# Outer buffers for three expert pairs, two single-use buffers, router rows in two blocks, and the pool scale spread by GpSimd

## What is computed

```python
def pool_mixer(x, pool_w, pool_scale):     # layer 0
    ...
    y = jnp.einsum("bsgc,gcd->bsgd", pooled, pool_w).reshape(B, S, D)
    return y * pool_scale                  # one factor for each of 2048 features

def hier_moe(...):                         # in both layers, 16 experts
    # router: top-1 group of 4, then top-2 of its 4 experts
    h = silu(einsum("td,edf->tef", xt, w_gate)) * einsum("td,edf->tef", xt, w_up)
    y = einsum("tef,efd->td", h * gate[:, :, None], w_down)
```

## Time and profile before

| | |
|---|---|
| median of 3 runs | 1384.12 us (1383.57 to 1386.93) |
| profiled execution, span | 1384.6 us |
| TensorE (PE) busy | 1344.2 us, 97% |
| VectorE (DVE) busy | 556.2 us, 40% |
| ScalarE (ACT) busy | 412.7 us, 30% |
| GpSimd (POOL) busy | 42.2 us, 3% |
| DMA | 481.80 MB, mean 348 GB/s |
| mean granted TensorE clock | 0.990 |

### The profile page before, as it was taken

How to read it: one execution, slowest core, us unless ns; L and a number is a source line. 1 busy time by engine, 2 the same in 40 slices (tenths; PEclk the granted TensorE clock), 3 DMA queues, 4 the chain that set the end, 5 groups by cost and what they waited for, 6 DMA issues and landing times.

```text
span 1384.6 us, 21994 instructions
## 1 busy us (share of the span) xinstructions
PE 1344.2 (97%) x9081; PEld 763.4 (55%) x9081; DVE 556.2 (40%) x906; ACT 412.7 (30%) x636; POOL 42.2 (3%) x35
## 2 busy tenths in 40 slices
PE   9899999999999999999999999999999999999997
PEld 8644444443334458888888877764444444334443
DVE  5813222232222246566665665552322323222223
ACT  5611111111101136665656565531111111111112
POOL 1200000000000000000000000110000000000000
PEclk9999999999999999999999999999999999999999
DMA  9999999999999999644545444579999999999997
GB/s 361 406 421 421 419 421 421 426 427 428 428 428 423 421 394 384 209 157 156 179 141 193 152 152 152 183 263 421 420 421 421 421 426 428 427 428 428 424 420 269
DMA packets 86657, 481.80 MB, mean 348 GB/s; under 512 B 6462, under 2 KB 6672, under 8 KB 47412
## 3 DMA queue, kind: packets, MB, share of 16 engines
q1 hardware_dynamic: 85988, 477.50, 85.7%
q10 hardware_dynamic: 432, 2.65, 0.5%
q0 software_dynamic: 160, 0.52, 0.1%
HBM read 478.56 MB, written 2.10 MB: 347 GB/s over the span
## 4 chain that ended last, share of the span: by engine, by line
issue 53%; PE 34%; DMA 7%; DVE 3%; POOL 1%; ACT 1%; SPq 1%; POOLq 0%; ACTq 0%; DVEq 0%
PE ps L1789 13%; PE ps L1597 7%; DMA ring<-in_moe_w_up 6%; PE ps L1827 5%; PE ps L1678 2%; PE ps L1843 2%; PE ps L1754 1%; PE ps L1755 1%; POOL head_rs L625 1%; DMA bias_row<-in_moe_b_rt 1%; DVE ws L1024 1%; PE ps L1882 1%; PE ps L1816 0%; DVE ps L1354 0%; DVE resid L1357 0%
## 5 line engine op out<-in xcount | busy, mean ns | idle before, releaser
L1789 PE MATMUL ps<-ring,xg 128*64 128x512 f32 x1664 | 388.2, 608 | 19.8 <-DMA ring<-in_moe_w_up 15.4
L1597 PE MATMUL ps<-ws,xs 128*128 128x512 f32 x1632 | 383.8, 393 | 2.6 <-DVE ws L1027 1.1
L1597 PEld LDWEIGHTS ps<-ws,xs 128*128 128x128 f32 x1632 | 304.0, 189 | 70.9 <-DVE ws L1027 3.6
L1789 PEld LDWEIGHTS ps<-ring,xg 128*64 128x64 f32 x1664 | 123.0, 139 | 255.0 <-issue 254.7
L1827 PE MATMUL ps<-ring,hidT 128*64 128x512 f32 x832 | 184.6, 595 | 0.0
L1027 DVE SCALAR_TENSOR_TENSOR ws<-ring,vecs,ws 128x512 fp32r<-128x512 f32 x192 | 134.3, 747 | 87.5 <-ACT ws L646 87.5
L1221 DVE TENSOR_TENSOR y_lo<-ps,y_hi 64x512 fp32r<-64x512 f32 x112 | 77.1, 688 | 191.6 <-ACT y_hi L710 188.9
L646 ACT ACTIVATE ws<-ring,vecs 128x512 fp32r<-128x512 f32 x192 | 127.3, 715 | 83.1 <-PE ps L1597 83.0
L1201 DVE TENSOR_TENSOR resid<-resid,ps 128x512 f32<-128x512 f32 x112 | 72.0, 684 | 170.8 <-PE ps L1755 170.8
L701 ACT ACTIVATE silu_g<-ps,slot_scale 64x512 f32<-64x512 f32 x28 | 19.1, 684 | 402.3 <-PE ps L1789 402.3
L710 ACT ACTIVATE y_hi<-ps 64x512 fp32r<-64x512 f32 x112 | 66.3, 592 | 209.2 <-PE ps L1827 207.2
(11 more groups left out here) (199 smaller groups left out, 825.0 us busy)
## 6 DMA issues: line engine op xcount, KB each, us to landing
ring<-in_moe_w_gate SPq DMA_DIRECT2D x72, 1024.0 KB, 13.9
ring<-in_moe_w_up SPq DMA_DIRECT2D x72, 1024.0 KB, 14.7
ring<-in_moe_w_down SPq DMA_DIRECT2D x72, 1024.0 KB, 15.0
ring<-in_moe_w_gate SPq DMA_DIRECT2D x24, 2048.0 KB, 15.7
ring<-in_moe_w_up SPq DMA_DIRECT2D x24, 2048.0 KB, 20.1
ring<-in_moe_w_down SPq DMA_DIRECT2D x24, 2048.0 KB, 18.5
ring<-in_w_kv SPq DMA_DIRECT2D x32, 1024.0 KB, 5.7
ring<-in_w_q SPq DMA_DIRECT2D x16, 1024.0 KB, 5.4
```

Of the source, the lines that this page charges most:

```text
L1597: last = mm(ps[:, bank + t, :], xs[:, px, k, cols], ws[:, b, pw, j, :], start=(first and j == 0 and n == 0), stop=(last_unit and j == 1 an ...
L1789: last = mm(ps[CAP * h:CAP * h + CAP, b, :], xg[:, b, k, :], both[h][:, j, :], start=(k == 0), stop=(k == KD - 1))
```

## The change

The outer buffers are used for three pairs (`PEELED` = 3, 72 loads). Two further buffers, `early`, take loads 6 and 7 of the layer, once; they lie at 0 to 8 KB and 16 to 24 KB, where `xs` holds the high and low half of the first eight tiles, and wait until these have been read (layer 0: four units used; layer 1: 28 of the O product's 32). The first round is thus 19 loads; loads 19 to 24 take the buffers of 0 to 5, load 25 that of load 8, and so on 17 back. The three outer buffers in `ws` wait each for its own last use. The fifth outer buffer (load 18) waits for the residual in layer 0 and is issued last of the first round; in layer 1 it is issued first, as soon as the third chunk of `oT` has been split. `xr` shrinks to 8 tiles, used alternately by blocks 0, 2 and 1, 3. `xg` and `y_hi` change places, `pick` moves. The pool scale comes by one DMA of 8 KB to one partition (`scale_src`), and GpSimd spreads each group over the partitions with `partition_broadcast`, at the places where it issued DMAs; the spreads of groups 0 and 1 stand behind the first norm's power.

```diff
-PEELED = 2
+PEELED = 3
...
+FIRST = WIDE + EARLY
+EARLY_LOADS = (6, 7)
+ROUND = [m for m in range(FIRST) if m not in EARLY_LOADS]
+BEFORE = {m: m - WIDE if m - FIRST >= WIDE else ROUND[m - FIRST] for m in range(FIRST, AHEAD)}
...
+OLD_XR = 18
+ISSUE_ORDER = [[0, 1, 2, 3, 4, 5, 8, 9, 10, 11, 12, *EARLY_LOADS, 13, 14, 15, 16, 17, OLD_XR],
+               [OLD_XR, 0, 1, 2, 3, 4, 5, 8, 9, 10, 11, 12, *EARLY_LOADS, 13, 14, 15, 16, 17]]
...
-        xr = at(56 * KB, "xr", [P, KD, SEQ])
+        xr = at(56 * KB, "xr", [P, 8, SEQ])
+        xr_all = at(56 * KB, "xr_all", [P, KD, SEQ])
...
-        xg = at(0, "xg", [P, 2, KD, CAP])
-        y_hi = at(8 * KB, "y_hi", [P, NBLK, BLK], F32R)
+        y_hi = at(0, "y_hi", [P, NBLK, BLK], F32R)
+        xg = at(8 * KB, "xg", [P, 2, KD, CAP])
...
+        early = [at(16 * KB * j, f"early{j}", [P, 2048]) for j in range(EARLY)]
...
+        EXTRA_BUFS = [extra[:, j, :] for j in (1, 2, 0, 3, 4)] + [early[j][:, :] for j in range(EARLY)]
+        LAST_UNITS = (UNIT_ATT, UNIT_O + 8 * NBLK)
+        XS_HALF_READ = (4, UNIT_O + 8 * (NBLK - 1) + 4)
+        def last_use(l, b):
+            return max(u for u in range(LAST_UNITS[l]) if u % UNIT_BUFS == b) + 1
...
-                for m in range(AHEAD):
+                for m in ISSUE_ORDER[l] + list(range(FIRST, AHEAD)):
                     e, part = m // SLOTS, m % SLOTS
                     if m in EXTRA_OF:
                         j, use = EXTRA_OF[m]
                         if use:
-                            sp.wait_ge(slot_read, NPAIR * PAIR_SLOTS * l + m - WIDE + 1)
-                        elif j == 0:
-                            sp.wait_ge(unit_used, (UNIT_ATT, UNIT_O + 8 * NBLK)[l])
+                            sp.wait_ge(slot_read, NPAIR * PAIR_SLOTS * l + BEFORE[m] + 1)
+                        elif j < WS_EXTRA:
+                            sp.wait_ge(unit_used, last_use(l, (1, 2, 0)[j]))
                         elif j == WS_EXTRA:
                             sp.wait_ge(route_mm, 4 * l + 1)
+                        elif j >= EXTRA:
+                            sp.wait_ge(unit_used, XS_HALF_READ[l])
+                        elif l:
+                            sp.wait_ge(xs_lo, 16 + 3)
+                        else:
+                            sp.wait_ge(resid_added, 8)
...
-            for g in range(2):
-                sp.dma_start(scale_row[:, g, :], pool_scale[:, g * BLK:(g + 1) * BLK].to_broadcast([P, BLK])).then_inc(scale_loaded[g], 16)
+            sp.dma_start(scale_src[:, :, 0:BLK], pool_scale.rearrange("a (g c) -> a g c", g=NG)).then_inc(scale_loaded, 16)
...
-            def load_scale(g):
-                pool.wait_ge(mixed_done, 2 * (g - 2) + 2)
-                pool.dma_start(scale_row[:, g % 2, :], pool_scale[:, g * BLK:(g + 1) * BLK].to_broadcast([P, BLK])).then_inc(scale_loaded[g], 16)
+            def spread_scale(g):
+                if g > 1:
+                    pool.wait_ge(mixed_done, 2 * (g - 2) + 2)
+                else:
+                    pool.wait_ge(scale_loaded, 16)
+                nc.gpsimd.partition_broadcast(scale_row[:, g % 2, :], scale_src[0:1, g, 0:BLK]).then_inc(scale_spread, 1)
...
             inverse_rms(0)
-            load_scale(2)
+            spread_scale(0)
+            spread_scale(1)
+            spread_scale(2)
             residual_parts(0, 0)
-            load_scale(3)
+            spread_scale(3)
             residual_parts(0, 1)
...
-                nc.scalar.activation(xr[:, 4 * c:4 * c + 2, :],
+                nc.scalar.activation(xr[:, 4 * (c % 2):4 * (c % 2) + 2, :],
...
-                    dve.wait_ge(scale_loaded[g], 16)
+                    dve.wait_ge(scale_spread, g + 1)
```

More of the change, by code:

```diff
@@ L36, with place_of, use_of @@
 EXTRA = 5
+EARLY = 2
 WIDE = SLOTS + EXTRA
-PEELED = 2
+PEELED = 3
 AHEAD = PEELED * PAIR_SLOTS
-EXTRA_USES = [sum(1 for m in range(AHEAD) if m % WIDE == SLOTS + j) for j in range(EXTRA)]
+FIRST = WIDE + EARLY
+EARLY_LOADS = (6, 7)
+ROUND = [m for m in range(FIRST) if m not in EARLY_LOADS]
+BEFORE = {m: m - WIDE if m - FIRST >= WIDE else ROUND[m - FIRST] for m in range(FIRST, AHEAD)}
+def place_of(m):
+    while m in BEFORE:
+        m = BEFORE[m]
+    return ("early", EARLY_LOADS.index(m)) if m in EARLY_LOADS else ("ring", None) if m < SLOTS + EARLY else ("extra", m - SLOTS - EARLY)
+PLACES = {m: place_of(m) for m in range(AHEAD)}
+EXTRA_USES = [sum(1 for m in range(AHEAD) if PLACES[m] == ("extra", j)) for j in range(EXTRA)] + [1] * EARLY
+def use_of(m):
+    return 1 + use_of(BEFORE[m]) if m in BEFORE else 0
+OLD_XR = 18
+ISSUE_ORDER = [[0, 1, 2, 3, 4, 5, 8, 9, 10, 11, 12, *EARLY_LOADS, 13, 14, 15, 16, 17, OLD_XR],
+               [OLD_XR, 0, 1, 2, 3, 4, 5, 8, 9, 10, 11, 12, *EARLY_LOADS, 13, 14, 15, 16, 17]]
 MOE_SLOTS = NPAIR * PAIR_SLOTS - sum(EXTRA_USES)
@@ L139, in build @@
         gain_rows = at(78 * KB, "gain_rows", [4, 8 * P])
-        bias_row = at(82 * KB, "bias_row", [1, 2, 20])
-        one_row = at(82 * KB + 256, "one_row", [1, P])
+        bias_row = at(65 * KB + 512, "bias_row", [1, 2, 20])
+        one_row = at(66 * KB, "one_row", [1, P])
+        scale_src = at(82 * KB, "scale_src", [1, NG, 2 * BLK])
         scale_row = at(68 * KB, "scale_row", [P, 2, BLK])
-        xr = at(56 * KB, "xr", [P, KD, SEQ])
+        xr = at(56 * KB, "xr", [P, 8, SEQ])
+        xr_all = at(56 * KB, "xr_all", [P, KD, SEQ])
         parts = at(72 * KB, "parts", [P, 3, NT, D], BF16)
@@ L164, in build @@
         hidT = at(20 * KB, "hidT", [P, 2, KF, CAP])
-        pick = at(22 * KB, "pick", [P, NT, 2, CAP], BF16)
+        pick = at(31 * KB, "pick", [P, NT, 2, CAP], BF16)
         logitsT = at(24 * KB, "logitsT", [P, SEQ])
@@ L212, in build @@
         slot_loaded = [sem(f"slot_loaded{j}") for j in range(SLOTS)]
-        extra_loaded = [sem(f"extra_loaded{j}") for j in range(EXTRA)]
+        extra_loaded = [sem(f"extra_loaded{j}") for j in range(EXTRA + EARLY)]
         slot_read = sem("slot_read")
@@ L236, in build @@
         tile0_done = sem("tile0_done")
-        scale_loaded = [sem(f"scale_loaded{j}") for j in range(NG)]
+        scale_loaded = sem("scale_loaded")
+        scale_spread = sem("scale_spread")
         mixed_done = sem("mixed_done")
@@ L322, in build @@
         for m in range(NPAIR * PAIR_SLOTS):
-            if m < AHEAD and m % WIDE >= SLOTS:
-                EXTRA_OF[m] = (m % WIDE - SLOTS, m // WIDE)
+            if m < AHEAD and PLACES[m][0] != "ring":
+                kind, j = PLACES[m]
+                EXTRA_OF[m] = (EXTRA + j if kind == "early" else j, use_of(m))
             else:
@@ L455, in moe @@
                         if use:
-                            sp.wait_ge(slot_read, NPAIR * PAIR_SLOTS * l + m - WIDE + 1)
-                        elif j == 0:
-                            sp.wait_ge(unit_used, (UNIT_ATT, UNIT_O + 8 * NBLK)[l])
+                            sp.wait_ge(slot_read, NPAIR * PAIR_SLOTS * l + BEFORE[m] + 1)
+                        elif j < WS_EXTRA:
+                            sp.wait_ge(unit_used, last_use(l, (1, 2, 0)[j]))
                         elif j == WS_EXTRA:
                             sp.wait_ge(route_mm, 4 * l + 1)
-                        row = extra[:, j, :]
+                        elif j >= EXTRA:
[4 more added lines that the diff above has]
+                            sp.wait_ge(resid_added, 8)
+                        row = EXTRA_BUFS[j]
                         sp.dma_start(row.rearrange("p (k c) -> p k c", k=4) if part < 8 else row,
@@ L1633, in route_block @@
                     col = 20 * (KD * l + k)
-                    last = mm(ps[32 * j:32 * j + 32, 6, 0:SEQ], w_route[:, col:col + 32], xr[:, k, :],
+                    last = mm(ps[32 * j:32 * j + 32, 6, 0:SEQ], w_route[:, col:col + 32], xr[:, 4 * (c % 2) + j, :],
                               start=(c == 0), stop=(c == NBLK - 1))
@@ L1939, in overflow @@
                                 for k in range(KD):
-                                    last = mm(ps[:, h, :], xr[:, k, t * P:(t + 1) * P], four(2 * (k // 4) + h)[:, k % 4, :],
+                                    last = mm(ps[:, h, :], xr_all[:, k, t * P:(t + 1) * P], four(2 * (k // 4) + h)[:, k % 4, :],
                                               start=(k == 0), stop=(k == KD - 1))
```

6 lines of the change are left out of this document (3 added, 3 removed).

## The result

The kernel after takes 1390.05 us (median of 8 runs, 1387.44 to 1391.32) where the kernel before, run beside it, takes 1385.36: the ratio is 1.0034, with an interval of 1.0025 to 1.0043. It is 4.7 us slower. The forecast was 6.8 us faster. One of the eight runs of before beside it took 1926.28 us; it counts as disturbed and isn't in the ratio. The profiled execution of after spans 1388.3 us.

The account below looks back on a forecast made before the run. The prediction took the DMA stream to bound both expert stages and TensorE attention. Gains of 3.1 + 4.0 - 0.3 = 6.8 us took the profiled 1384.6 to 1377.8, the median to 1377.3; range 1375.3 to 1382.3.

Parts of the forecast that it names:

- (a): Expert stages: two more buffers, used once each, let TensorE find 19 slots loaded; capped gains of 3.1 and 4.0 us.
- the cap: Load 25 can't land before load 8's buffer release plus 5.2 us, limiting the gain to 3.1 and 4.0 us.
- (b): Stage one: dropping the scale's four broadcast DMAs saves 2.5 us of stream, not added, only letting the stage reach the cap.
- (c): Expert stages: outer buffers for a third pair keep 17 buffers until load 72, preventing losses of 1.2 or 0.3 us.
- (d): Mixer: GpSimd spreads the scale at 1.5 us per operation; contention with VectorE costs 0.3 us of the gain.
- their cover up to 5 us a spread: Mixer: GpSimd's 5.07 us of idle time was to hide the delay of `residual_parts` queued behind each spread.
- (e): Router rows, swapped places, early buffers in `xs`, issue order: addresses only, costing nothing, at most one latency of 5.2 us.
- R3: Rival: the spread needs code not loaded, 8 to 12 us, delaying VectorE's first use 2 to 6 us; chance 0.10.
- R1: Rival: the lead leaks behind load 8 through late single loads; gain only 3 to 5 us, about 1380.2; chance 0.17.
- R4: Rival: the spread's code transfer queues behind the full DMA stream, some 18 us late, 1395; chance 0.05.
- R2: Rival: experts start earlier as less stands in the mixer's way; gain 9 to 10 us, 1375; chance 0.06.
- R5: Rival: nothing gained, because TensorE was the bound after all; 1384; chance 0.06.

Follow-up runs that it names:

- e1_buffers: The kernel after, with the pool scale brought by broadcast DMAs as in the kernel before; 1384.61 us, ratio 0.9996.
- e3_one_swap: The kernel after, with all four spreads of the scale in a row, each into a row of its own; 1383.31 us, ratio 0.9988.
- e5_three_pairs: The kernel before with `PEELED` = 3 and nothing else, so the outer buffers serve three pairs; ratio 1.0008.
- e6_alternate: e3_one_swap plus small alternating broadcasts and additions on GpSimd, six rounds behind the mixer, two before the O products; span 1380.7 us against 1381.5.

## Why the prediction was wrong, step by step

**What bounds the kernel.** Right for the expert stages and attention. Left out was the mixer: the forecast took the first expert product as fixed "at 63.47" with a delay of 0.3, and it moved by +5.28 in after (and by -1.99 in e1_buffers, within what equal mixers differ by). What follows stage one carries a late start one for one: the O product's last units start at 912.31 instead of 906.90.

**(a) The early buffers and the cap.** The mechanism was right. Load 25 was issued at 90.19, which is 84.91 + 5.28, and at 954.26, which is 948.84 + 5.42, and landed 4.9 us later each time (the forecast: 5.2). Against the shifted start the stages gained 3.5 and 4.4 us at that load; the sum had 3.1 and 4.0. The step that failed is "Behind load 25 the stream is continuous", and with it the sum's "each shift goes through whole". It had 0.7 us to spare at load 26. But the load issued next, at 955.98, needed 7.0 us to land, not 5.2, and a lead won by running the queue empty also wiped out the spread that, by my reading, hides late shares. In stage two 1.6 of 4.4 us reached TensorE's end. In all, the sum's 7.1 us for the buffers measured 0.6.

In stage one after gained nothing. By its landings 1.7 us were left of the 3.5 (last load 510.93 against 507.37, with the start 5.28 later), and TensorE ended 5.4 us later than before. There the granted clock stood at half (the 1.2 GHz level) for 3.4 us from 440.8 on, behind one of TensorE's last waits in the stage (2.66 us), and 32 records of the gate and up products took 8.78 us for 7.09. No wait for weights came behind it, so these 1.7 us could not be made up. In before the last such stretch was at 398.8, and TensorE still waited 0.60 us for weights at 501.87: it had caught up by then.

In e1_buffers stage one did not reach the cap at all: its load 25 landed at 92.3, where 93.3 is before's, since its stream, with the scale's bytes in it, ran without a stop until then and could not be sooner. A first product 2 us earlier found no weights earlier behind the stock. Its landings then fell from 1.1 to 3.3 us behind before's, counted from the first product, which stays open.

**(b) The scale's bytes.** Right: load 16 landed at 67.0 in after and 66.5 in e3_one_swap, for 69.8; the forecast said 67.3. It is worth nothing by itself, as said. e3_one_swap is 1.3 us faster than e1_buffers with it, which is not clear of noise.

**(c) Outer buffers for the third pair.** Mis-sized: the losses that they were to prevent were 1.2 and 0.3 us, together 1.5, in the forecast. With the early buffers they are worth 1388.83 - 1384.61 = 4.2 us, since without them the distance falls by five places at load 48. Without the early buffers they cost 1.1 (-0.1 to 2.2). "contained in the sums of (a)" was right in kind, but it made the whole of (a) hang on them.

**(d) The spread on GpSimd.** The operation was within its bounds (0.80 us in the median, 1.44 at the most in after, for 1.5). The step that failed is "their cover up to 5 us a spread": it priced the operation, and not what its neighbours on GpSimd have to pay for having it between them. The bound of 7.0 us was of the right size, but it was applied to the first spread alone (where it is hidden, as the forecast said) and not to the change back. Contention with VectorE, the 0.3, was not the term that mattered: e3_one_swap has the same four broadcasts and is under before. The wait went where the forecast did look, at `residual_parts` queued behind. There the cover was 5.07 + 2.86 us, and three changes in a row took 22.9; 5.3 us were left at the first expert product, and 5.4 in the time.

**(e) Addresses, order of the issues.** Nothing was seen of them; no run took them apart.

**The sum and the median.** The device time of a run of after is its span + 2.0 to 2.2 us in all eight runs. The profiled execution of before, 1384.6, was then a run of 1386.8, above the median of 1384.12, and not one 0.5 above it as I wrote. The differences don't hang on it, but trace comparisons with that execution flatter a change by up to 2 us: e5_three_pairs has a span 2.2 below it and a median 0.08% above.

**The rivals.** R3 and R1 both happened, and the forecast had let each stand alone. R3 named the cause, code that isn't loaded, with 8 to 12 us; the records MODIFY_POOL_CONFIG at every change speak for it, though what is loaded the trace doesn't show. Its place was wrong: the first use, hidden until 27.3, instead of the three changes behind it. So its 2 to 6 us were the right size (5.4) by a wrong path, and its 1379 to 1383 still counted the gain of 6.8. R1 had the leak with "single loads come a microsecond or two late now and then", and a gain of 3 to 5; the buffers gave 0.6 with the old scale, 1.7 in e3_one_swap. R4 would be some 3 us of a change in e6_alternate, if that is queueing, and not 18. R2 did not occur. R5 has nearly the number that the buffers alone reached, but not the reason: TensorE still idled 9.1 and 11.7 us in the two stretches above.

## What to carry to other kernels

A PARTITION_BROADCAST among ordinary operations on GpSimd is to be priced per change of kind, there and back, and not per operation: here 6 to 9 us each, 7 to 12 beside a full DMA stream. The trace marks each with MODIFY_POOL_CONFIG on GpSimd's sequencer; look for these records first. Put all broadcasts together, where nothing is queued behind them: four in a row cost this kernel nothing that shows, the same four at two places 5 us.
More buffers in front of a stream that is the bound are worth what is left of the lead when the queue next runs dry, not what they hold. Buffers used once give their lead back at the first release they don't take part in: follow the distance in places over the whole stage, and allow one late landing (1.0 to 1.4 us here) for each stop.

## What the runs showed of the hardware

- A change between PARTITION_BROADCAST and TENSOR_TENSOR on GpSimd took 5.9 to 8.6 us beside half-idle DMA and 6.8 to 12.3 us beside a full stream, at every one of 16 changes, and each began with two records MODIFY_POOL_CONFIG. A broadcast of 512 float32 to 128 partitions took 0.80 us in the median.
- Fetches of instructions take time from the weights. With eleven more packets of 8 KB the landings fell back by 6.3 us, as one of the 16 completions of a load fell back with each. They came from 3500 waits that had nothing to wait for, on an engine that was otherwise idle.
The Trainium skill (Runtime: NRT & Kernel Launch, Instruction fetch mechanics) calls the cost of crossing a block of code "mostly hidden". What it costs the engine that runs the code no run here shows; the weights beside it paid, and the kernel took 5.0 us more.
